# A two-layer hybrid decoder on one Trainium2 core: loads and order of the opening, and the column pieces of the last gates

## The reference, cut to what matters

```python
h = x                                                     # x: 256 tokens x 1024, f32
for i in range(2):
    f = swiglu(rmsnorm(h, ffn1_pre_g[i]), ffn1_w_in[i], ffn1_w_down[i])    # 1024 -> 2816 -> 1024
    h = h + 0.5 * rmsnorm(f, ffn1_post_g[i])
    hn = rmsnorm(h, mix_pre_g[i])
    mixed = hybrid gMLP + Mamba-2 SSD of hn (i = 0) or latent attention of hn (i = 1)
    h = h + rmsnorm(mixed, mix_post_g[i])
    f = swiglu(rmsnorm(h, ffn2_pre_g[i]), ffn2_w_in[i], ffn2_w_down[i])
    h = h + 0.5 * rmsnorm(f, ffn2_post_g[i])
    gate = sigmoid(rmsnorm(h, ple_pre_g[i]) @ ple_w_gate[i])               # 1024 x 1024
    h = h + rmsnorm(gate * (p[i] @ ple_w_proj[i]), ple_post_g[i])
return h
```

## Time and profile before

| | |
|---|---|
| median of 3 runs | 1111.8 us (1111.53 to 1111.99) |
| the profiled execution's own time | 1111.49 us |
| its span, first to last instruction | 1109.8 us |
| PE busy | 1099.7 us, 99% |
| PEld, DVE, ACT, POOL busy | 935.9, 814.1, 569.3, 83.8 us |
| granted TensorE clock, mean | 0.998 |

### The profile page before, as it was taken

The page is one execution under the profiler, slowest core; times in us unless marked ns, Lnnn a source line. Parts: engine busy times, 40 slices in busy tenths (PEclk is TensorE's granted clock), DMA queues, the critical chain, the costliest instruction groups (busy, mean ns, idle before and its releaser), DMA issues.

```text
span 1109.8 us, 14118 instructions
## 1 busy us (share of the span) xinstructions
PE 1099.7 (99%) x5719; PEld 935.9 (84%) x5719; DVE 814.1 (73%) x1074; ACT 569.3 (51%) x706; POOL 83.8 (8%) x138
## 2 busy tenths in 40 slices
PE   9999999999999999999999999999999999999997
PEld 6888888887888888888888888888898888888886
DVE  5777777588997677677786866768876667766775
ACT  7534434567564554444565444346775555444454
POOL 2300000200110200000113000001200020000011
PEclk9999999999999999999999999999999999999999
DMA  8755555645544565555555555554523365555541
GB/s 324 249 190 190 190 190 186 250 173 188 185 176 152 206 221 190 190 190 190 190 198 219 197 190 192 191 188 172 206 81 110 120 251 184 193 190 193 193 165 57
DMA packets 31600, 208.37 MB, mean 188 GB/s; under 512 B 3760, under 2 KB 3808, under 8 KB 8112
## 3 DMA queue, kind: packets, MB, share of 16 engines
q1 hardware_dynamic: 27792, 193.48, 49.6%
q0 software_dynamic: 3600, 13.46, 3.5%
q10 hardware_dynamic: 144, 0.52, 0.1%
HBM read 206.39 MB, written 1.06 MB: 187 GB/s over the span
## 4 chain that ended last, share of the span: by engine, by line
PE 93%; DVE 2%; issue 1%; DMA 1%; ACT 1%; POOL 0%; SPq 0%; DVEq 0%; POOLq 0%
PE PS L737 24%; PE PS L186 17%; PE PS L188 17%; PE PS L187 17%; PE PS L734 12%; PE PS L383 1%; DMA raw<-stream 1%; PE PS L1957 1%; DVE WL L168 1%; PE PS L1254 1%; PE PS L1978 1%; ACT WH L161 1%; PE PS L1959 0%; PE PS L1968 0%; DMA h<-x 0%
## 5 line engine op out<-in xcount | busy, mean ns | idle before, releaser
L168 DVE TENSOR_TENSOR WL<-raw,WH 128x2048 fp32r<-128x2048 f32 x180 | 411.1, 2289 | 158.9 <-ACT WH L161 158.9
L161 ACT ACTIVATE WH<-raw 128x2048 fp32r<-128x2048 f32 x180 | 342.8, 1907 | 82.8 <-DMA raw<-stream 82.5
L737 PE MATMUL PS<-X,WH 128*128 128x512 f32 x1152 | 276.0, 391 | 0.0
L737 PEld LDWEIGHTS PS<-X,WH 128*128 128x128 f32 x1152 | 213.1, 188 | 42.2
L841 ACT ACTIVATE sgb<-sgb 128x256 f32<-128x256 f32 x72 | 30.0, 417 | 263.6 <-DVE sgb L837 263.6
L734 PEld LDWEIGHTS PS<-X,WL 128*128 128x128 f32 x1152 | 143.5, 192 | 3.1
L734 PE MATMUL PS<-X,WL 128*128 128x256 f32 x1152 | 144.5, 283 | 0.0
L186 PE MATMUL PS<-WH,X 128*128 128x512 f32 (+3 forms) x360 | 141.0, 392 | 0.8 <-DVE WL L168 0.4
L188 PE MATMUL PS<-WL,X 128*128 128x512 f32 (+3 forms) x360 | 138.7, 385 | 0.0
L187 PE MATMUL PS<-WH,X 128*128 128x512 f32 (+3 forms) x360 | 138.5, 385 | 0.0
L186 PE MATMUL PS<-WH,BH 128*128 128x512 f32 x288 | 113.3, 393 | 0.0
(11 more groups left out here) (280 smaller groups left out, 1314.8 us busy)
## 6 DMA issues: line engine op xcount, KB each, us to landing
raw<-stream SPq DMA_DIRECT2D x181, 1024.0 KB, 4.8
PG<-post_g POOLq DMA_DIRECT2D x8, 512.0 KB, 6.7
QG<-pre_g POOLq DMA_DIRECT2D x7, 512.0 KB, 7.6
Eg<-acs_rows POOLq DMA_DIRECT2D x2, 1024.0 KB, 5.9
raw<-stream SPq DMA_DIRECT2D x3, 512.0 KB, 6.3
h<-x SPq DMA_DIRECT2D x4, 256.0 KB, 4.3
out<-h SPq DMA_DIRECT2D x4, 256.0 KB, 2.0
raw<-stream ACTq DMA_DIRECT2D x1, 512.0 KB, 4.3
```

What stands on the lines that cost most here:

```text
L161: act.activation(WH[:, n % RING, :], raw[:, n % RING, :], ACT.Copy).then_inc(sem("w_hi"), 1)
L168: dve.tensor_tensor(WL[:, n % RING, :], raw[:, n % RING, :], WH[:, n % RING, :], ALU.subtract).then_inc(sem("w_lo"), 1)
L737: ins = pe.matmul(PS[:, bank, :], wh[:, kt, cols], X[:, kt, :, :].rearrange("p a n -> p (a n)"), start=opens, stop=closes, skip_group_chec ...
```

## The change

Two places and two small edits.

1. Loads. SP no longer waits for x before its next load, so that all loads of the opening are issued one behind the other. Unit 0 comes in three loads (256, 256 and 512 KB) instead of two (512, 512), the first two from ACT. `qg_cols` is issued by POOL.
2. Pieces. The second half of unit 0 is split in two pieces (nine pieces in all, not eight). On ACT and DVE the first weight piece stands ahead of x, and the first two quarters of tile 1 ahead of quarters 2 and 3 of tile 0. Each of the first quarters has a semaphore step of its own. Quarter 0 of x goes to another PSUM bank, and ACT waits for DVE's quarter 0 before it goes on to quarter 2.
3. PE. The first four groups of three products (`first_terms`) wait for each operand apart. Tile 1 is turned behind the first three products. All four groups go ahead of the turn of the second halves. Eight products of zeros instead of fifteen (7 and 1), from a smaller tile.
4. End. The last gates are cut at 512, 768 (512, 256, 256 columns). The squares of the last two pieces are DVE's, by a `tensor_tensor_reduce` that starts from the sum so far, instead of ACT's squares and DVE's last sum.
5. The 144 waits on `b_gsum` and `b_usum` are on the common `dve_chain`.

The diff, cut:

```diff
-            return PS[:, 6 + t if a_ == 0 and q > 1 else x_bank(0, t, a_), q * P:(q + 1) * P]
+            return PS[:, 6 + t if a_ == 0 and q != 1 else x_bank(0, t, a_), q * P:(q + 1) * P]
...
+                if (a_, q) == (0, 2):
+                    act.wait_ge(sem("x_lo_piece"), 2 * t + 1)
...
-        LOADS = [(0, 0, 1024), (0, 1024, 2048), (1, 0, 1024), (1, 1024, 2048)]
-        PARTS = [(0, 0, 512), (0, 512, 1024), (0, 1024, 2048), (1, 0, 512), (1, 512, 1024), (1, 1024, 2048),
-                 (2, 0, 1024), (2, 1024, 2048)]
+        LOADS = [(0, 0, 512), (0, 512, 1024), (0, 1024, 2048), (1, 0, 1024), (1, 1024, 2048)]
+        PARTS = [(0, 0, 512), (0, 512, 1024), (0, 1024, 1536), (0, 1536, 2048),
+                 (1, 0, 512), (1, 512, 1024), (1, 1024, 2048), (2, 0, 1024), (2, 1024, 2048)]
...
+            def first_terms(t, q):
+
+                bank = PS[:, (A, B)[t], :]
+                pe.wait_ge(sem("w_part_hi"), q + 1)
+                pe.wait_ge(sem("x_piece"), 2 * t + q + 1)
+                pe.matmul(bank, tokens(XH, 0, t, q), weights(WH, 0, q), start=q == 0, stop=False)
+                pe.wait_ge(sem("x_lo_piece"), 2 * t + q + 1)
+                pe.matmul(bank, tokens(XL, 0, t, q), weights(WH, 0, q), start=False, stop=False)
+                pe.wait_ge(sem("w_lo_half"), q + 1)
+                pe.matmul(bank, tokens(XH, 0, t, q), weights(WL, 0, q), start=False, stop=False)
...
+            first_terms(0, 0)
+            transpose_x(pe, 0, 1, (0,))
+            first_terms(0, 1)
+            first_terms(1, 0)
+            first_terms(1, 1)
+            transpose_x(pe, 0, 0, (1,))
...
-                for lo, hi, out_ap in ((0, 512, PS[:, 2, :]), (512, 896, PS[:, 3, 0:384]), (896, 1024, PS[:, 0, 0:P])):
+                for lo, hi, out_ap in ((0, 512, PS[:, 2, :]), (512, 768, PS[:, 3, 0:SEQ]), (768, 1024, PS[:, 0, 0:SEQ])):
...
-                act.activation(junk[:, c], gsb[:, 1, c], ACT.Square, scale=1.0 / 32, accum_out=col(s, 1, LAST_SQ[k]))\
-                   .then_inc(sem("post_sq"), 1)
...
+                ins = dve.tensor_tensor_reduce(out=junk[:, c], in0=gsb[:, 1, c], in1=gsb[:, 1, c], scale=1.0 / D,
+                                               scalar=col(s, 1, (POST_SQ, LAST_SUM[0])[k]), op0=ALU.mult, op1=ALU.add,
+                                               accum_out=col(s, 1, LAST_SUM[k]))
...
-            dve.tensor_scalar(col(s, 1, POST_RS), col(s, 1, POST_RS), col(s, 1, LAST_SQ[0]), col(s, 1, LAST_SQ[1]),
-                              ALU.add, ALU.add).then_inc(sem("post_ms"), 1)
...
-            sp.dma_start(qg_cols[:, :], a["pre_g0"]).then_inc(sem("qg_cols"), 16)
-            sp.wait_ge(sem("x_in00"), 16)
-            load_part(sp, 1)
+            load_part(sp, 2)
             load_x(0, 1)
             load_x(1, 1)
-            load_part(sp, 2)
             load_part(sp, 3)
+            load_part(sp, 4)
...
+            pool.dma_start(qg_cols[:, :], a["pre_g0"]).then_inc(sem("qg_cols"), 16)
...
             load_part(act, 0)
+            load_part(act, 1)
```

More of the change, by code:

```diff
@@ L101, in hybrid_trunk @@
         end = 229344
-        zeros = place("zeros", [P, BANK], bf16, offset=s_at)
+        zeros = place("zeros", [P, P], bf16, offset=s_at)
         sg = place("sg", [P, 2, CHUNK], offset=s_at)
@@ L133, in sem @@
             return sems[name]
[L135 removed]
+        for name in ("raw0", "raw1", "raw2", "raw3", "raw4", "w_hi", "w_lo", "w_used", "x_in00", "x_in01", "x_in10", "x_in11", "zeros", "consts", "pg", "qg", "qg_cols", "w_part0", "w_part1", "w_part2", "w_part3", "w_part4", "x_piece", "x_lo_piece", "w_part_hi", "w_lo_half",
                      "out_done", "ple_done", "post_sq", "post_ms", "post_y", "post_rs", "h_new", "pre_sq", "pre_rs", "hn_done",
                      "x_tr", "x_hi", "x_lo", "gate", "silu", "up", "acted", "h_tr", "h_hi", "h_lo",
[L138 removed]
+                     "rs_tr", "rs_there", "b_gate", "b_scaled", "b_silu", "b_act", "b_hi", "b_lo",
                      "dve_chain", "pool_chain", "stored"):
@@ L430, in first_x_low @@
                 kt = 4 * a_ + q
-                if (a_, q) == (0, 0):
-                    dve.wait_ge(sem("x_piece"), t + 1)
+                if a_ == 0 and q < 2:
+                    dve.wait_ge(sem("x_piece"), 2 * t + q + 1)
                 elif q == 2 * (1 - a_):
@@ L436, in first_x_low @@
                                                qg_cols[:, kt:kt + 1], XH[:, kt, tok(t)], ALU.mult, ALU.subtract)
-                if (a_, q) == (0, 1):
+                if a_ == 0 and q < 2:
                     ins.then_inc(sem("x_lo_piece"), 1)
@@ L590, in opening_dve @@
         def opening_dve(dve, done):
+            first_part_lo(dve, 0)
             first_x_low(dve, 0, 0, (0, 1))
-            first_part_lo(dve, 0)
             first_part_lo(dve, 1)
+            first_x_low(dve, 1, 0, (0, 1))
             first_x_low(dve, 0, 0, (2, 3))
-            first_x_low(dve, 1, 0)
             first_part_lo(dve, 2)
+            first_part_lo(dve, 3)
+            first_x_low(dve, 1, 0, (2, 3))
             first_x_low(dve, 0, 1)
-            first_part_lo(dve, 3)
+            first_part_lo(dve, 4)
             first_x_low(dve, 1, 1)
-            for i in range(4, 8):
+            for i in range(5, 9):
                 first_part_lo(dve, i)
@@ L629, in opening_pe @@
         def opening_pe(pe):
[L631 to L654, removed]
@@ new lines, in weights, with tokens @@
+            def weights(tile, j, q):
+                return whole(tile, j).rearrange("p (k n) -> p k n", k=4)[:, q, :]
+            def tokens(tile, j, t, q):
+                return tile[:, 4 * j + q, tok(t)]
+            def first_terms(t, q):
[7 more added lines that the diff above has]
+                pe.matmul(bank, tokens(XH, 0, t, q), weights(WL, 0, q), start=False, stop=False)
@@ new lines, in terms @@
+            def terms(j, t, q):
+                return product(pe, PS[:, (A, B)[t], :], tokens(XH, j, t, q), tokens(XL, j, t, q),
+                               weights(WH, j, q), weights(WL, j, q), False, (j, q) == (1, 3))
+            first_terms(0, 0)
[4 more added lines that the diff above has]
+            transpose_x(pe, 0, 0, (1,))
+            for t in range(2):
+                x_there(pe, 0, t, 0)
+                if t == 0:
+                    pe.wait_ge(sem("w_lo_half"), 3)
+                terms(0, t, 2)
+                if t == 0:
+                    split_done(pe, 0)
+                ins = terms(0, t, 3)
+                if t == 0:
+                    transpose_x(pe, 0, 1, (1,))
@@ new lines, in opening_pe @@
+            ins.then_inc(sem("w_used"), 1)
+            for part in range(2):
+                for t in range(2):
+                    x_there(pe, 0, t, 1)
+                    for q in (2 * part, 2 * part + 1):
+                        if (part, t) == (0, 0):
+                            pe.wait_ge(sem("w_lo_half"), 4 + q)
+                        elif t == 0:
+                            split_done(pe, 1)
+                        ins = terms(1, t, q)
+                    if part:
+                        ins.then_inc(sem("w_used" if t else "gate"), 1)
@@ L2444, in idle_products @@
             for _ in range(n):
-                pe.matmul(PS[:, A, :], zeros[:, 0:P], zeros[:, :], start=True, stop=True)
+                pe.matmul(PS[:, A, :].rearrange("p (k n) -> p k n", n=P), zeros[:, :],
+                          zeros[:, :].unsqueeze(1).broadcast_to([P, 4, P]), start=True, stop=True)
         @block.tensor
```

53 lines of the change are left out of this document (26 added, 27 removed).

## The result

| | before | after |
|---|---|---|
| median of 20 runs each, us | 1111.75 (1110.97 to 1112.3) | 1113.67 (1112.14 to 1114.7, and one stray of 2843.37) |
| ratio after to before, 95% interval | | 1.0019 (1.0013 to 1.0026) |
| profiled execution's own time, span | 1111.49, 1109.8 | 1113.48, 1111.7 |
| start of the 28th product | 15.96 | 18.21 |
| first product of the second column piece to first update of h | 9.10 | 8.19 |

Three executions far above all others (2843.37 here, 1212.49 in e10, 1643.33 among those of before beside e1 to e4) are left out of the ratios, not of the medians.

A forecast was written before the change was run, and what follows sets the result against it. PE is busy 1099.7 of 1109.8 us, so only opening and end can gain: 1111.49 - 0.55 - 1.05 = 1109.9 for the profiled execution, 1110.2 us as median forecast (0.14% faster); own range 1109.8 to 1110.6, 8 in 10 range 1109.2 to 1112.1.

The forecast's parts named there:

- The opening: Up to the 28th product (k-tile 1 of unit 1): it starts at 15.4 instead of 15.96, gain 0.55 us.
- Landing between 5.2 and 6.9 ... I take 0: qg_cols (4 KB) on POOL's queue: ACT wants it at 6.15, so it costs 0 to 0.75 us, taken as 0.
- rival 2: Opening: clock rises at 8 to 9, or qg_cols lands at 6.9, taking the opening's gain: 1110.8 us; chance 0.18.
- Less in the range, not in the sum: PE's clock in the opening: rise at about the same time or up to 1.5 us later; 0.1 off in the range only.
- rival 1: Opening: PE's clock rises late, at 11.7; 28th product at 17.4, 1.45 later than before; 1112.2 us; chance 0.20.
- turns do not hold the clock up: PE's opening, from the Trainium skill: turns don't count as PE work for the clock as products do, so the rise is later.
- The order: New queue of ACT, DVE and PE in the opening: ACT's first quarter at 6.15, 28th product at 15.4.
- Loads in a row: SP's opening loads without the wait: those behind come 1.5 us or more earlier; unit 1's first half lands at about 11, off the path.
- The end: Last gates in 256-column pieces, from the products to POOL's power: gain 1.05 us, between 0.9 and 1.15.
- The middle: Between opening and end: 144 renamed waits cost 0; units 2 and 3 follow 0.55 earlier with 0.5 us margin on DVE, 0.

The follow-up runs named there:

- e10: Kernel before with 8 products of zeros (7, 1 and none) instead of 15, nothing else; median 1112.25 us, ratio 1.0004.
- e1: Changed kernel with the gains (qg_cols) issued by SP as its third transfer again, not by POOL; median 1113.47 us, ratio 1.0015.
- e4: Kernel before with the new end only (columns 512, 256, 256 and VectorE's sum); median 1110.73 us, ratio 0.9991.
- e2: Changed kernel with 9 and 8 products of zeros instead of 7 and 1, gains still on POOL; median 1111.84 us, ratio 1.0002.
- e3: Changed kernel with the gains on SP and 9 and 3 products of zeros; median 1112.08 us, ratio 1.0005.
- e9: Changed kernel with SP's wait for x of tile 0 put back and 9 and 8 products of zeros; median 1111.28 us, ratio 0.9997.
- e6: Changed kernel with SP's wait for x of tile 0 put back, gains on POOL, 7 and 1 products of zeros; median 1111.96 us, ratio 1.0001.
- e7: Kernel before with SP's wait for x of tile 0 taken out, nothing else; median 1111.13 us, ratio 0.9996.
- e11: Kernel before without SP's wait for x of tile 0 and with the new end; median 1110.63 us, ratio 0.9992.
- e5: Changed kernel with the gains issued first by ACT, ahead of its weight loads, and 9 and 3 products of zeros; median 1112.74 us, ratio 1.0006.

## Why the prediction was wrong, by its steps

**The opening: forecast 15.4, measured 18.21, off by 2.81.** The profiles divide it. Late gains: the first quarter at 7.34, not 6.15, +1.19. The clock: 10.87 less the 9.60 of e2, e3 and e9, +1.27. The order itself: 9.60 less the forecast's 9.25 (15.4 less 6.15), +0.35. Sum 2.81.

**"Landing between 5.2 and 6.9 ... I take 0".** This is the step that failed first. The landing was 7.31, outside my bounds. The lower bound came from the gains of before, for which SP held its loads back, and the change takes just that away. The upper one came from a POOL load of 16 KB that is issued at 25.73, in other traffic, and was no bound for this one. I let the loads in a row speed up what is behind them and left what is ahead as it was., which I read as a hole to be filled, can be read the other way: the 82 GB/s at 5 to 6 us were the far side of the room in which x, the gains and the first weights came home. x of tile 0 landed at 5.06 (4.87), the turn followed at 5.09: there I was nearly right, since x is issued first. e1, e3 and e6 show that the price hangs on what else is in flight and not on the issuing engine. The third load of unit 0 may be a part of it: without the wait and from SP the gains took 4.77 and 5.18 us with unit 0 in two loads (e7, e11), 5.44 and 5.63 with three (e1, e3). No run changes that alone.
The Trainium skill (DMA: Bandwidth & Descriptors, Queues, rings and completion order) says that a DMA engine takes turns between the queues it has work for, one packet at a time, and under Issuing engines are not separate DMA queues that all issuers share the same 16 engines. These runs agree with the second: 5.98 us from POOL, 5.44 and 5.63 from SP. They don't show the turns, and that a load alone on POOL's queue took 5.98 us, while one first on ACT's took 2.7, is not explained by them. The 0.4 us of the issuing path, which I weighed in rival 2, is small beside this.

**"Less in the range, not in the sum": the clock.** It rose early enough in after (the turn at 5.09 took 0.63), so rival 1's picture of a late rise is not what happened there; it fell behind a rest of 1.92 us that the late gains made, and one product of zeros did not cover. This is the second step that failed: the term stood at 0 in the sum, with 0.1 in the range, and measured 1.27. The mechanism is the one that I worked out for rival 1: ACT waits for a slow tile 1's turn, and the second-half turn stands behind twelve products (12.79; I had 12.7). In e6, with the gains in time, the rise came late as in rival 1, at about 10.0, with the 28th product at 16.97 (17.4 there). So rival 1 had the right mechanism, given 0.20, and rival 2 the other half, given 0.18; I treated as alternatives two things that came together. That turns do not hold the clock up, which I cited against the change, no run here separates from plain rest.

**The order.** In e9 ACT's queue reaches tile 1's second half at 13.06; forecast 12.35. 0.26 is the first quarter, about 0.45 the waits on PE: ACT's row at 8.43 says 0.87 idle behind the turn (0.55 in the forecast), which starts 0.86 after the first product (7.79 less 6.93), not 0.7.

**Loads in a row.** Unit 1's first half did leave the path, as forecast, in all runs without the wait. But this buys nothing that e7 and e11 can tell from noise.

**The end.** Forecast 1.05, range 0.9 to 1.15, measured 0.91 in the profile of after and in e4's median: inside the range, at its low edge, for POOL's power. That the median hits the same 0.91 is chance, its interval being 1 us.

**The middle, which I priced at 0: +0.64.** 0.36 of it is one place, in all seven kernels with the new opening and in none of the seven others: the attention stage at 779 us, where PE waits for DVE's cTL 0.53 to 0.59, else 0.15 to 0.24. The chain there in after, POOL then DVE, and in before:

```profile
775.33 0.30 POOL L2327 TENSOR_SCALAR msm<-msm,stat 128x2 f32<-128x2 f32 x1
776.07 0.48 DVE L2210 SCALAR_TENSOR_TENSOR cn<-PS,msm,cg 128x256 f32<-128x256 f32 x1 [0.46 <-POOL msm L2327]
```

```profile
772.76 0.30 POOL L2298 TENSOR_SCALAR msm<-msm,stat 128x2 f32<-128x2 f32 x1
773.15 0.48 DVE L2181 SCALAR_TENSOR_TENSOR cn<-PS,msm,cg 128x256 f32<-128x256 f32 x1
```

DVE starts 0.44 after POOL's end, in before 0.09. Why an instruction 760 us behind the edit starts late stays open; nothing in the trace holds it. The other 0.28 is within what profiles of one middle differ by: from the 28th product to PE's last start, with the end's 1.06 (6.70 less 5.64) added back where it applies, the seven kernels with the old opening have 1087.06 to 1088.36, before's own profile 1087.52, and the seven with the new one 1087.55 to 1088.29, after 1088.16. So the late start is in every kernel of the new order, but the 0.64 as a whole is no more than the spread.

## What to carry to other kernels

A wait that holds loads back may be what lets the first, needed transfers land. When it goes, price every transfer issued in the same microseconds again, the smallest ones too: their latency in the old profile was measured in the old traffic. And products of zeros are cover for what may come late; count them against the latest time at which the operand may come, not the expected one, above all where turns stand in PE's queue behind real products and another engine waits for the turns.

## What was not expected of the hardware

- A 4 KB load took 2.7 us (first on ACT's queue), 4.1 to 4.5 (third on SP's, with the wait), 4.9 and 5.1 (POOL, with the wait), 4.8 to 5.2 (SP, no wait), 5.4 to 6.0 (no wait, unit 0 in three loads).
- The clock fell after rests of 0.88 and 1.92 us with a turn and one product of zeros between them (after), and after 0.68 and 1.51 with two turns and one product of zeros between (e10); both times the slow stretch that followed had PE busy throughout. It did not fall behind a rest of 1.03 with three products of zeros ahead of it (e3), nor behind rests of 1.07 and 0.83 (e5).
- The first rise wanders: with 7 products of zeros it had come by 5.09 in after, while in e6, with the same products, PE was at the slow level until about 10.0. So one profile of an opening does not fix its clock.
